# Fourier stage, first part: the next tile's join between centring and scaling, folds in pairs, GpSimd's roots in another order

## Chip, core and metric

The kernel runs on one core of a Trainium2 chip. The metric is the time of one execution in device microseconds; lower is better. The engines are TensorE (PE in the profile), VectorE (DVE), ScalarE (ACT), GpSimd (POOL) and SyncE (SP), which issues most transfers. Each engine works off its own queue of instructions in order and waits for others by semaphores.

## What is computed

Two layers of a diffusion trunk on 1024 tokens of width 1024, each with a token mixer and a mixture of experts. Layer 0 mixes by windowed attention, layer 1 by a Fourier transform. The change is in the Fourier stage of layer 1, and in its first part only. What that part computes, for x of 1024 x 1024:

```python
def post_norm(x, y, g, b):                     # end of layer 0: y is the summed output of its experts
    z = DEEPNORM_ALPHA * x.astype(jnp.float32) + y.astype(jnp.float32)
    return (_normalize(z, LN_EPS) * g.astype(jnp.float32) + b.astype(jnp.float32)).astype(x.dtype)

def modulate(x, shift, scale):                 # start of layer 1
    return (_normalize(x, MOD_EPS) * (1.0 + scale.astype(jnp.float32)) + shift.astype(jnp.float32)).astype(x.dtype)

def fourier_mixer(u, w_f):
    B, L, D = u.shape
    ug = u.reshape(B, L, F_GROUPS, D // F_GROUPS).astype(jnp.float32)
    f = jnp.fft.fft2(ug, axes=(1, 3), norm='ortho').real
    return f.reshape(B, L, D).astype(u.dtype) @ w_f

        x = post_norm(x, g2 * y2, ln_g[i, 1], ln_b[i, 1])
        u = modulate(x, sh1, sc1)
        y = fourier_mixer(u, fnet_w[j])
```

## The kernel before

The tokens lie in eight tiles of 128 rows. `TURN` orders them so that tiles 2j and 2j + 1 of the order are those whose rows are half the sequence apart; the transform over the tokens works on their sum and difference. All loops are unrolled, and the order of the instructions on each engine is the order in which they are written out. For tile i of the order the first part does this:

- SP: `load(i)` fetches the two partial sums of the experts from memory into one of three buffers `y[i % 3]`; from the fourth on it waits until that buffer has been read.
- TensorE: `total(i)` adds the partial sums into the one PSUM area `psY` (L278; for the first two tiles L276 too); it waits until the tile before has been joined.
- VectorE: *join* (L2189) forms z = ALPHA * x + psY in the one buffer `z`; *statistics* (L2190 to L2193) end with the variance, on which GpSimd's `root1` (L2147) works; *centring* (L2194) is (z - mean) * gain; *scaling* (L2196) waits for the root and writes x, with the row sums.
- ScalarE: `mean(i)` (L2256, L2258) takes the mean from these sums and the sum of squares; GpSimd's `root2` (L2152, L2154) makes the second root of it in two instructions; `normal(i)` (L2263, L2265) writes u, one of four buffers.
- VectorE: `fold(k)` (L2182) writes the sum (k even) or the difference (k odd) of the two u of a pair into `pm`; both folds of a pair want both u.
- TensorE: `turn(k)` (L2344) transposes a fold into the one area `psT`; ScalarE: `turned(k)` (L2270) copies it out; TensorE: `features(k)` (L2355) multiplies it by the feature table, in two halves; ScalarE: `features(k)` (L2275) copies each half to F.

Between these stands work on the condition's rows: TensorE's `rows(q)` and `columns()`, on ScalarE `rows(q)` (a copy, L2237 to L2242, for q = 1, 2 with a transfer issued from ScalarE's queue, L2245), `columns()` (L2227 to L2231, which scales the feature table that features(0) reads) and `spread`. The last tile's u is made on VectorE (`normalise`, L297 to L304). The second part (from L2383 on) multiplies F by the token tables and begins when all of F is there.

VectorE's order before is: for tile i join, statistics, centring, scaling, fold(i - 2). GpSimd's is: root2(i - 1), then root1(i). ScalarE's for tile i is: mean(i), columns at i = 1, turned(i - 2), normal(i), features(i - 3), rows(i - 1) at i = 2 and 3. TensorE's from i = 2 on is: total(i + 1), rows(2) at i = 2, turn(i - 2), features(i - 3).

## Time and profile before

| what | us |
|---|---|
| median of 3 runs (2733.79 to 2737.6) | 2733.92 |
| the profiled execution, its own time | 2736.14 |
| its span, first to last instruction | 2734.3 |
| Fourier stage in it, 1545.0 to 1663.6 | 118.6 |
| its first part, until the last features matmul ends | 1545.0 to 1624.6 |
| TensorE busy in the whole span | 2622.8 (96%) |
| VectorE busy in the whole span | 2021.4 (74%) |

The times of single instructions below count from the start of the span. In the views of instructions in order of time a line gives the start, the duration, the engine, the line of the kernel, the operation, the tile written and the tiles read; in brackets stands the idle time of the engine just before it and the engine that ended it. `f_banks` is the PSUM, `f_feat` is F or `pm`, `wide_t` holds z and u, `f_ny` and `wide_w` hold what was transposed.

### The profile page before, as it was taken

How to read it: one execution, taken by the hardware profiler on the slowest of the kernel's cores; microseconds unless marked ns; L12 is line 12 of the kernel's file. 1: busy time of each engine (PE TensorE's matmuls, PEld its weight loads, DVE VectorE, ACT ScalarE, POOL GpSimd, SP SyncE). 2: the span in 40 equal slices, each digit the busy share in tenths (PEclk: the TensorE clock that was granted, in tenths of full speed). 3: DMA queues.
4: the chain of work that ended last, by engine and by line, in shares of the span. 5: the costliest groups of instructions: out<-in, count | busy, mean ns of one | idle time of the engine just before them, and what ended most of it. 6: DMA issues, size and time to landing. Idle time of an engine off the chain costs nothing. (4 is left out here: it accounts for less than half of the span.)

```text
span 2734.3 us, 44521 instructions
## 1 busy us (share of the span) xinstructions
PE 2622.8 (96%) x14898; PEld 1188.5 (43%) x14899; DVE 2021.4 (74%) x5305; ACT 1367.1 (50%) x3178; POOL 615.0 (22%) x467
## 2 busy tenths in 40 slices
PE   7999999999899999999999889998999999999996
PEld 2444666545433333333444365454333333333342
DVE  4996666585588888788888555755898888888875
ACT  1113666343166666666666241432666666666651
POOL 0000000111023333233322221100233323333322
PEclk9999999999999999999999999999999999999998
DMA  9776500200399999999999732015999999999996
GB/s 376 253 267 198 187 17 17 76 39 39 130 378 367 335 333 353 324 334 377 353 337 335 253 138 88 34 47 228 356 363 345 334 320 338 331 377 336 331 356 206
DMA packets 151614, 697.66 MB, mean 255 GB/s; under 512 B 25504, under 2 KB 30880, under 8 KB 99161
## 3 DMA queue, kind: packets, MB, share of 16 engines
q1 hardware_dynamic: 104252, 556.14, 52.1%
q0 software_dynamic: 46832, 136.58, 20.2%
q8 instruction: 119, 1.95, 0.3%
q10 hardware_dynamic: 304, 2.11, 0.2%
q14 instruction: 107, 0.88, 0.1%
HBM read 597.50 MB, written 129.13 MB: 266 GB/s over the span
## 5 line engine op out<-in xcount | busy, mean ns | idle before, releaser
L1811 ACT ACTIVATE xT<-xt_blocks 32x256 f32<-32x256 f32 x2208 | 913.6, 414 | 40.2 <-DVE xt_blocks L1636 12.6
L1888 PE MATMUL exG<-ring,xT 128*32 128x512 f32 (+2 forms) x2608 | 572.2, 594 | 0.8 <-DMA ring<-in_exp_w_up_dram 0.8
L1651 DVE STREAM_TRANSPOSE ex_hT<-ex_h 32x64 f32<-32x64 f32 x2240 | 528.7, 236 | 33.6
L1888 PE MATMUL exG<-wide_w,xT 128*32 128x512 f32 (+2 forms) x1472 | 387.5, 601 | 0.0
L1561 POOL DMA_INDIRECT y_scratch<-wide_w,idx_out x203 | 337.2, 1661 | 165.0 <-issue 80.1
L1888 PE MATMUL exG<-wide_t,xT 128*32 128x512 f32 (+2 forms) x960 | 360.2, 602 | 11.2 <-issue 7.6
L1548 POOL DMA_INDIRECT wide_t<-u_scratch,idx x144 | 152.8, 1061 | 923.7 <-DVE idx_out L1685 779.1
L1888 PEld LDWEIGHTS exG<-ring,xT 128*32 128x32 f32 (+2 forms) x2608 | 199.3, 130 | 315.9 <-issue 311.7
L1823 ACT ACTIVATE ex_e<-exG 128x256 f32<-128x256 f32 x142 | 54.4, 383 | 513.7 <-PE exG L1888 513.7
L1922 PE MATMUL exD<-ring,ex_hT 128*32 128x512 f32 (+2 forms) x1304 | 296.2, 597 | 2.6 <-DVE wide_w L1677 2.5
L1641 DVE TENSOR_TENSOR ex_h<-ex_e,exG 128x256 f32<-128x256 f32 x142 | 86.9, 612 | 167.3 <-ACT ex_e L1823 165.0
L1888 PEld LDWEIGHTS exG<-wide_w,xT 128*32 128x32 f32 (+2 forms) x1472 | 133.6, 135 | 147.6 <-issue 147.6
L1922 PE MATMUL exD<-wide_w,ex_hT 128*32 128x512 f32 (+2 forms) x736 | 197.4, 597 | 0.0
L1677 DVE SCALAR_TENSOR_TENSOR wide_w<-exD,w_all,mod 128x1024 f32<-128x1024 f32 x142 | 182.3, 1284 | 9.4 <-PE exD L1922 8.4
L1888 PEld LDWEIGHTS exG<-wide_t,xT 128*32 128x32 f32 (+2 forms) x960 | 111.3, 136 | 166.8 <-issue 163.3
L1922 PE MATMUL exD<-wide_t,ex_hT 128*32 128x512 f32 (+2 forms) x480 | 182.0, 597 | 0.0
L1600 DVE TENSOR_TENSOR mod<-place,slots 128x1024 bf16<-128x1024 f32 (+3 forms) x203 | 175.2, 889 | 5.0 <-PEq L235 3.6
L1636 DVE STREAM_TRANSPOSE xt_blocks<-wide_t 128x1024 f32<-128x1024 f32 x138 | 170.8, 1237 | 1.6 <-DMA wide_t<-u_scratch,idx 1.6
L795 DVE TENSOR_REDUCE mx<-pair 128x1 f32<-128x640 f32 (+1 forms) x128 | 100.6, 787 | 94.4 <-PE pair L923 94.4
L315 POOL TENSOR_TENSOR rstd<-var,halves 128x1 f32<-128x1 f32 x42 | 62.9, 1498 | 441.1 <-DVE var L301 441.1
L1922 PEld LDWEIGHTS exD<-ring,ex_hT 128*32 128x32 f32 (+2 forms) x1304 | 97.0, 129 | 116.8 <-issue 115.6
L1241 ACT ACTIVATE u2T<-mod 32x256 f32<-32x256 f32 x224 | 92.7, 414 | 107.1 <-DVE mod L1115 104.5
(367 smaller groups left out, 3293.8 us busy)
## 6 DMA issues: line engine op xcount, KB each, us to landing
ring<-in_exp_w_gate_dram SPq DMA_DIRECT2D x64, 1024.0 KB
ring<-in_exp_w_up_dram SPq DMA_DIRECT2D x64, 1024.0 KB
ring<-in_exp_w_down_dram SPq DMA_DIRECT2D x64, 1024.0 KB, 14.2
wide_t<-in_exp_w_gate_dram SPq DMA_DIRECT2D x34, 1024.0 KB
wide_t<-in_exp_w_up_dram SPq DMA_DIRECT2D x34, 1024.0 KB
wide_t<-in_exp_w_down_dram SPq DMA_DIRECT2D x34, 1024.0 KB, 14.5
wide_w<-in_exp_w_gate_dram SPq DMA_DIRECT2D x32, 1024.0 KB
wide_w<-in_exp_w_up_dram SPq DMA_DIRECT2D x32, 1024.0 KB
```

Source lines behind the costliest of these rows:

```text
L795: dve.tensor_reduce(mx[:, p % 2, j:j + 1], halves_of(p, pair[p % 2])[j], AX, ALU.max).then_inc(own, 1)
L1241: last = act.activation(uT[m * UNIT:(m + 1) * UNIT, t % DEEP, :, a * UNIT:(a + 1) * UNIT], parts[a * UNIT:(a + 1) * UNIT, m], ACT.Copy)
L1548: pool.indirect_dma_start(out=xg[:, par], out_offset=None, in_=u_dram, in_offset=bass.IndirectOffsetOnAxis(ap=idx[:, par:par + 1], axis=0) ...
L1561: pool.indirect_dma_start(out=y_dram[layer], out_offset=bass.IndirectOffsetOnAxis(ap=idx_out[0:at + n, par, j:j + 1], axis=0), in_=yo[0:at ...
L1600: last = dve.tensor_tensor(hot[:, par, :, at:at + n], place[:, :, r:r + 1].to_broadcast([P, NT, n]), slots[:, start:start + n].unsqueeze(1 ...
L1636: dve.transpose(xt[:], xg[:, par]).then_inc(blocks_done, 1)
L1641: dve.tensor_tensor(hid[:, par].rearrange("t (k p) -> t p k", k=FK), e[:].rearrange("t (p k) -> t p k", k=FK), psG[par][:, 1].rearrange("t ...
L1651: last = dve.transpose(hT[m * UNIT:(m + 1) * UNIT, par].rearrange("p (k t) -> p k t", k=FK)[:, :, a * UNIT:(a + 1) * UNIT], hid[a * UNIT:( ...
L1677: dve.scalar_tensor_tensor(out=yo[:, par], in0=psD[:].rearrange("p a b -> p (a b)"), scalar=w_all[:, ds(b, 1)], in1=gate2, op0=ALU.mult, o ...
L1811: last = act.activation(xT[m * UNIT:(m + 1) * UNIT, par, :, a * UNIT:(a + 1) * UNIT], parts[a * UNIT:(a + 1) * UNIT, m], ACT.Copy)
L1888: last = pe.matmul(psG[par][p:p + m], xT[:, par, k, p:p + m], ring[s % RING][:, 0:2, k * FF:(k + 1) * FF], start=k == 0, stop=k == KT - 1)
L1922: last = pe.matmul(psD[p:p + m, c], hT[:, b % 2, k * P + p:k * P + p + m], ring[s % RING][:, 2, k * D + c * 512:k * D + (c + 1) * 512], st ...
```

## The change

VectorE now joins tile i + 1 between the centring and the scaling of tile i (for i = 1 behind the scaling). For this z has two buffers, and the row of the bias that lay in one of them moves to the last u buffer. Two semaphores, `z_joined` and `z_mid`, replace two of the four links per tile. The folds come in pairs behind the scaling of tiles 2, 4 and 6. GpSimd does root1(i) ahead of root2(i - 1). SP issues load(3) ahead of sums(2) and load(4) ahead of the tables. ScalarE's queue goes by pairs: mean(i), turned(i - 2), normal(i), turned(i - 1), features(i - 2), then mean(i + 1), normal(i + 1), features(i - 1); both columns() and the first two tiles' normal come ahead of it, rows(1) and rows(2) behind features(0). TensorE's goes by pairs too: turn(k), total(k + 4), turn(k + 1), features(k), total(k + 5), features(k + 1).

```diff
-                z, u, pm = fT[:, 3], fT[:, 4:4 + U], F[:, 6:8]
+                z, u, pm = [fT[:, 0], fT[:, 3]], fT[:, 4:4 + U], F[:, 6:8]
...
-                bias_a, bias_b = fT[:, 0], F[:, 1:6].rearrange("p t d -> p (t d)")
+                bias_a, bias_b = fT[:, 7], F[:, 1:6].rearrange("p t d -> p (t d)")
...
                         load(2)
+                        load(3)
                         sums(2)
-                        load(3)
+                        load(4)
                         for buf, name in ((even_c, "even_c"), (odd_c, "odd_c"), (even_s, "even_s")):
                             sp.dma_start(buf[:].rearrange("p a b -> p (a b)"), A[name]).then_inc(t_in, 16)
-                        for i in range(4, NT):
+                        for i in range(5, NT):
                             load(i)
...
                         add_last(pool, layer, held)
-                        for i in range(NT):
-                            if i >= 1:
-                                root2(i - 1)
+                        root1(0)
+                        for i in range(1, NT):
                             root1(i)
+                            root2(i - 1)
                         root1(NT)
...
-                        for i, t in enumerate(TURN):
-                            link = Links(dve, own, i * 4)
-                            after(dve, x_done, i, 1)
+                        def joined(i):
+
                             dve.wait_ge(y_mm, i + 1)
-                            xs = x[:, t]
-                            link(stt(out=z, in0=xs, scalar=ALPHA, in1=flat(psY), op0=ALU.mult, op1=ALU.add))
-                            dve.bn_stats(r["st"][:, 0, :], z[:, 0:512])
-                            link(dve.bn_stats(r["st"][:, 1, :], z[:, 512:1024]))
+                            at_least(dve, x_done, i - 1)
+                            stt(out=z[i % 2], in0=x[:, TURN[i]], scalar=ALPHA, in1=flat(psY), op0=ALU.mult, op1=ALU.add).then_inc(z_joined, 1)
+
+                        def centred(i):
+
+                            link = Links(dve, own, i * 2)
+                            dve.wait_ge(z_joined, i + 1)
+                            dve.bn_stats(r["st"][:, 0, :], z[i % 2][:, 0:512])
+                            link(dve.bn_stats(r["st"][:, 1, :], z[i % 2][:, 512:1024]))
                             link(dve.bn_aggr(r["mv"][:], r["st"][:]))
                             dve.tensor_scalar(r["var"][:], r["mv"][:, 1:2], LN_EPS, None, ALU.add).then_inc(r["asked"], 1)
-                            link(stt(out=z, in0=z, scalar=r["mv"][:, 0:1], in1=lnp[:, 0], op0=ALU.subtract, op1=ALU.mult))
+                            stt(out=z[i % 2], in0=z[i % 2], scalar=r["mv"][:, 0:1], in1=lnp[:, 0], op0=ALU.subtract, op1=ALU.mult).then_inc(z_mid, 1)
+
+                        def scaled(i):
+
+                            dve.wait_ge(z_mid, i + 1)
                             dve.wait_ge(r["ready"], i + 1)
-                            stt(out=xs, in0=z, scalar=r["rstd"][:], in1=lnp[:, 1], op0=ALU.mult, op1=ALU.add, accum_out=sm[:, i:i + 1]).then_inc(x_done, 1)
-                            if i >= 2:
+                            stt(out=x[:, TURN[i]], in0=z[i % 2], scalar=r["rstd"][:], in1=lnp[:, 1], op0=ALU.mult, op1=ALU.add,
+                                accum_out=sm[:, i:i + 1]).then_inc(x_done, 1)
+
+                        joined(0)
+                        for i in range(NT):
+                            centred(i)
+                            if i != 1 and i + 1 < NT:
+                                joined(i + 1)
+                            scaled(i)
+                            if i == 1:
+                                joined(2)
+                            if i >= 2 and i % 2 == 0:
                                 fold(i - 2)
-                            assert link.n == 4
+                                fold(i - 1)
...
                         rows(0)
-                        for i in range(NT):
-                            if i < NT - 1:
-                                mean(i)
-                            if i == 1:
-                                columns()
+                        for i in range(2):
+                            mean(i)
+                            normal(i)
+                        columns()
+                        for i in range(2, NT, 2):
+                            mean(i)
+                            turned(i - 2)
+                            normal(i)
+                            turned(i - 1)
+                            features(i - 2)
+                            if i == 2:
+                                rows(1)
+                                rows(2)
                             if i == 6:
                                 spread(1)
                                 spread(2)
-                            if i >= 2:
-                                turned(i - 2)
-                            if i < NT - 1:
-                                normal(i)
-                            if i >= 3:
-                                features(i - 3)
-                            if i in (2, 3):
-                                rows(i - 1)
+                            if i + 1 < NT - 1:
+                                mean(i + 1)
+                                normal(i + 1)
+                            features(i - 1)
                         turned(NT - 2)
-                        features(NT - 3)
                         turned(NT - 1)
...
-                            if i >= 1:
-                                pe.wait_ge(own, 4 * (i - 1) + 1)
+                            at_least(pe, z_joined, i)
                             add_sums(pe, psY, pairs, y[i % 3], layer, TURN[i], held).then_inc(y_mm, 1)
...
-                        for i in range(2, NT):
-                            if i + 1 < NT:
-                                total(i + 1)
-                            if i == 2:
-                                rows(2)
-                            turn(i - 2)
-                            if i >= 3:
-                                features(i - 3)
+                        total(3)
+                        rows(2)
+                        for k in range(0, NT - 2, 2):
+                            turn(k)
+                            if k + 4 < NT:
+                                total(k + 4)
+                            turn(k + 1)
+                            features(k)
+                            if k + 5 < NT:
+                                total(k + 5)
+                            features(k + 1)
                         turn(NT - 2)
-                        features(NT - 3)
                         turn(NT - 1)
```

## Rows read from the trace of the kernel before

**Rows 1.** Busy us of each engine by stretches; then granted clock, DMA share, GB/s.
```profile
1565.00:1607.00 42.00, 34.42 (x176) 20.14 (x168) 36.85 (x54) 29.78 (x52) 12.91 (x17) 0.95 0.51 194
1607.00:1625.00 18.00, 16.81 (x88) 14.50 (x88) 5.44 (x8) 7.64 (x11) 0.55 (x1) 1.00 0.00 0
...
1579.00:1581.00 2.00, 2.00 (x9) 1.73 (x7) 1.92 (x4) 1.33 (x3) 0.55 (x1) 0.53 0.10 38
```

**Rows 2.** Waits from 1545 to 1610: who for whom, us, times, longest.
```profile
DVE x L2196 <- POOL rstd L2147: 4.9, 8, 1.3
```

**Rows 3.** VectorE in order of time: join of tile 2; tile 6, join to fold.
```profile
1563.86 1.22 DVE L2189 SCALAR_TENSOR_TENSOR wide_t<-x,f_banks 128x1024 f32<-128x1024 f32 x1 [1.18 <-PE f_banks L278]
...
1593.59 1.21 DVE L2189 SCALAR_TENSOR_TENSOR wide_t<-x,f_banks 128x1024 f32<-128x1024 f32 x1
...
1596.47 1.28 DVE L2194 SCALAR_TENSOR_TENSOR wide_t<-wide_t,mean_var,wide_w 128x1024 f32<-128x1024 f32 x1
1598.26 1.28 DVE L2196 SCALAR_TENSOR_TENSOR x<-wide_t,rstd,wide_w 128x1024 f32<-128x1024 f32 x1 [0.51 <-POOL rstd L2147]
...
1599.47 1.22 DVE L2182 TENSOR_TENSOR f_feat<-wide_t 128x1024 f32<-128x1024 f32 x1
```

**Rows 4.** GpSimd in order of time: root2 and root1; the last root1.
```profile
1594.13 0.19 POOL L2152 TENSOR_SCALAR u_ss<-u_ss 128x1 f32<-128x1 f32 x1 [2.99 <-ACT wide_t L2258]
1594.41 0.55 POOL L2154 TENSOR_TENSOR u_rstd<-u_ss,halves 128x1 f32<-128x1 f32 x1
1596.64 1.52 POOL L2147 TENSOR_TENSOR rstd<-var,halves 128x1 f32<-128x1 f32 x1 [1.68 <-DVE var L2193]
...
1609.52 0.55 POOL L2147 TENSOR_TENSOR rstd<-var,halves 128x1 f32<-128x1 f32 x1 [4.35 <-DVE var L301]
```

**Rows 5.** All engines in order of time, in the finish stage.
```profile
2726.28 1.29 DVE L2032 SCALAR_TENSOR_TENSOR fx<-fz,z_rstd,mod 128x1024 f32<-128x1024 f32 x1
2726.38 1.59 POOL L2009 TENSOR_TENSOR z_rstd<-z_ss,halves 128x1 f32<-128x1 f32 x1
```

**Rows 6.** ScalarE in order of time: columns, rows' issues, mean, turned, normal, features.
```profile
1565.25 3.30 ACT L2231 ACTIVATE feat_scaled<-feat,f_scale 128x256 f32<-128x256 f32 x8
...
1575.44 1.07 ACTq L2245 DMA_DIRECT2D row_scratch<-odd_s  x1
...
1585.82 0.49 ACTq L2245 DMA_DIRECT2D row_scratch<-odd_s  x1
...
1592.57 0.20 ACT L2256 ACTIVATE u_nmean<-u_sum 128x1 f32<-128x1 f32 x1 [1.01 <-DVE x L2196]
1592.80 1.15 ACT L2258 ACTIVATE wide_t<-x,u_nmean 128x1024 f32<-128x1024 f32 x1
...
1594.86 1.02 ACT L2270 ACTIVATE wide_w<-f_banks 128x1024 f32<-128x1024 f32 x1 [0.81 <-PE f_banks L2344]
1595.78 0.29 ACT L2263 ACTIVATE u_shift<-u_nmean,u_rstd 128x1 f32<-128x1 f32 x1
1596.10 1.24 ACT L2265 ACTIVATE wide_t<-x,u_shift,u_rstd 128x1024 f32<-128x1024 f32 x1
1597.25 0.57 ACT L2275 ACTIVATE f_feat<-f_banks 128x512 f32<-128x512 f32 x1
```

**Rows 7.** TensorE in order of time: total(3), turns, features, and the second part's start.
```profile
1567.06 1.94 PE L278 MATMUL f_banks<-wide_w,pairs 128*64 128x512 f32 x8
...
1578.35 1.26 PE L2344 MATMUL f_banks<-ident,f_feat 128*128 128x128 f32 x8 [3.61 <-DVE f_feat L2182]
1579.39 5.18 PE L2355 MATMUL f_banks<-feat_scaled,f_ny 128*128 128x256 f32 x16
...
1607.76 1.09 PE L2344 MATMUL f_banks<-ident,f_feat 128*128 128x128 f32 x8 [2.47 <-DVE f_feat L2182]
...
1620.95 3.62 PE L2355 MATMUL f_banks<-feat_scaled,wide_w 128*128 128x256 f32 x16
1625.35 1.03 PE L2383 MATMUL f_banks<-even_c,f_feat 128*4 128x257 f32 x4 [0.78 <-ACT f_feat L2275]
```

More of the change, by code:

```diff
@@ L2099, in fourier @@
                 paired, y_mm, own, x_done = (sem(n) for n in ("paired", "y_summed", "fin_own", "x_done"))
+                z_joined, z_mid = sem("z_joined"), sem("z_mid")
                 y_in, ln_in = summed_in[layer], norm_in
```

## The prediction, made before the result was known

> **What bounds the kernel now.** I first read the busy time by stretches [rows 1]. The Fourier stage runs from 1545 to 1663.6 us of the span. In its first part, from 1565 to 1607, VectorE is busy 36.85 of 42 us and TensorE 34.42; from 1607 to 1625 VectorE has 5.44 of 18 left and TensorE 16.81. So the first part goes at VectorE's pace and hands over to a TensorE tail. Everything behind waits for the last features matmul, which starts at 1620.95 and ends at 1624.57: the second part's first matmul, at 1625.35, was released by ScalarE's copy of it [rows 7]. A microsecond there is a microsecond of the whole.
>
> Next VectorE's steady tile in order of time [rows 3]: join at 1593.59, behind it the statistics, centring at 1596.47, a wait of 0.51 for GpSimd's root, scaling at 1598.26, fold at 1599.47. From start to start that is 2.88 for join and statistics (1.22 of it the join), 1.79 for centring with the wait, 1.21 for scaling, and some 1.15 for the fold: 7 us a tile. The table of waits puts all eight root waits at 4.9 us [rows 2]. That is what the change can take away, at 0.5 to 0.6 a tile; it is no large prize.
>
> Why does the root take so long? It takes 1.52 while centring runs beside it (1596.47 to 1597.74, root until 1598.16) and 0.55 when nothing does [rows 3, 4]. The finish stage shows the same for a scaling: GpSimd starts at 2726.38, the scaling at 2726.28 ends at 2727.57, and the root takes 1.59, until 2727.97 [rows 5]. A root that meets centring or scaling ends 0.41 after that instruction. The sum below uses this.
>
> The Trainium skill ("SBUF — State Buffer", Who interferes with whom) says that a VectorE instruction with two SBUF inputs and a GpSimd one that reads SBUF exclude each other, whoever came first. GpSimd as the loser is in the rows; VectorE as the loser is not shown by any. By that rule scaling of tile 5 would be held about 0.1 more and the sum would be 3.7 instead of 3.6.
>
> **The parts of the change and their cost.** I lay the queues out in their new order with durations of the rows. TensorE: total 1.94, turn 1.09, features 3.62 [rows 7]. ScalarE: mean 1.5 (copy at 1592.57, square from 1592.80, GpSimd following at 1594.13), turned 1.02, normal 1.55 (1595.78 to 1597.34), each half of the features copy 0.6, eight column scalings 3.3 with two small ones of 0.2 in front of them [rows 4, 6]. GpSimd's second root: 0.83 from 1594.13 to its end at 1594.96 [rows 4]. Handing over from engine to engine costs 0.03 to 0.12. The same layout with the old orders gives 1624.4 for the last features matmul, against 1624.57 in the trace, so it is good to some 0.2 us.
>
> *Removed and nearly free.* The link waits in the join and centring cost nothing once another instruction stands between. The second z buffer and the bias row's new place cost nothing: only the first row sums read that bias, ahead of total(2), and its place, u of tile 3, is first written at about 1585 in the sum below. On SP load(3) passes sums(2), and load(4) passes the tables. This costs nothing: total(3) at 1567.06 shows no wait for a transfer [rows 7], rows(2), which reads sums(2), comes behind total(3), and total(4) comes 0.9 later than in the layout of the old orders. The row staging moves back to 1584.8, and the load of the last table, which waits for it on SP, with it; the table is wanted behind the last features matmul, 40 us later, and those 40 us are the cover. Without it the whole delay of the staging would count.
>
> *Tiles 2 and 3.* Join(2) still waits for data until 1563.86 [rows 3]. Centring ends at 1568.0. Join(3) now wants total(3) before scaling(2), but that ends at 1567.06 + 1.94 = 1569.0: VectorE waits 1.1, where it waited 0.51 for the root. Scaling(2) ends at 1571.6, folds 0 and 1 at 1573.8, join(4) and scaling(3) at 1579.2. The statistics of tile 4 start at 1579.0, against 1579.5 in the layout of the old orders. Gain so far 0.5.
>
> *Tiles 4 and 5.* On ScalarE normal(1) ends at 1570.8: its root2 stands behind root1(2) on GpSimd, which is held by centring until 1568.4. Behind it come columns (to 1574.4), mean(2) (to 1575.8) and turned(0) (to 1576.9), which before stood in another order. TensorE's turn(1) waits for turned(0), so features(0) runs 1577.8 to 1581.5 and total(5), behind it in the new order, ends at 1583.2. Centring(4) ended at 1581.9, so join(5) waits 1.5. Scaling(4) ends at 1585.9. Now the costly step: fold(2) needs u of tile 3, whose mean is queued on ScalarE behind features(0) (copied by 1582.1) and the two row stagings with their transfer issues (two copies of 0.6, issues of 1.07 and 0.49 [rows 6]; to 1584.8). Mean(3) ends at 1586.3, root2 at 1587.2, normal(3) at 1588.8. Fold(2) starts at 1588.85: VectorE waits 2.9. Queued behind it are fold(3), centring(5), and for TensorE turn(2).
>
> *Tiles 6 and 7.* From 1588.85 two folds (to 1591.2), centring(5), join(6) and scaling(5) to 1596.5, centring(6) to 1599.3, total(7) just in time, scaling(6) 1600.55 to 1601.9. On ScalarE normal(4) ends at 1596.9 (root2(4) waits for root1(5), which centring holds until 1594.4), turned(3) at 1597.8, the copies of features(2) at 1598.9, mean(5) at 1600.3. Its second root reaches the power at 1600.7, in the middle of scaling(6), and ends at 1602.3; normal(5) ends at 1603.9. Fold(4) starts at 1604.0: VectorE waits 2.0.
>
> *Tail.* Folds 4 and 5 end at 1606.3, root1(7) at 1609.55, scaling(7) at 1611.0, the last normalisation lets fold(6) start at 1614.4. Root2(6) stands behind root1(7), and its power is then held by scaling(7): 1611.4. Normal(6) ends at 1613.0, turned(5) behind it at 1614.0, one copy of features(4) at 1614.5; only then features(5) runs, to 1618.15. Turn(6), turned(6) and turn(7) end at 1621.3, features(6) and (7) at 1628.2. Sum: 1628.2 - 1624.57 = 3.6 us later.
>
> In short: tiles 2 to 6 give back their root waits, some 3, and a join wait of the old order goes (1.3 in its layout); the new waits (1.1, 1.5, 2.9, 2.0) take 7.5; the tail adds a little. Unknown costs: the power under scaling (nothing to 1.1 on each of three: held nowhere, the layout gives 1.6 later instead of 3.6; with no holding even by centring, 1.1 earlier); the transfer issue on ScalarE (0 to 1.6: 0.6 less if nothing). I take the held value, since its row is the same form of instruction [rows 5].
>
> The profiled execution took 2736.14 around a span of 2734.3; its sum becomes 2739.7. The median of the three runs is 2733.92, lower by 2.2, and I add the 3.6 to it: 2737.5.
>
> **Rivals.** (A) The sum: 2737.5, with 2735.5 to 2738.5 for the unknown costs.
>
> (B) GpSimd's new order doesn't bind, because the second roots come before the first ones ask. The layout with the old order of roots shows what that is worth: normal(1) is done at 1566, fold(2) at 1587.7, features(5) at 1609.2, and the end is 1.5 earlier than before: 2732.4. For it: a second root is 0.83 long and mostly idle time surrounds it. Against: root1 of the next tile is asked about 2 us after scaling and centring then holds it, so it must come first by order.
>
> (C) The other side, clearly slower: TensorE's clock. After a pause of 3.61 us turn(1) took 1.26 and features(0) 5.18 instead of 3.62 [rows 7], the granted clock being 0.53 (between its levels of 2.4 and 1.2 GHz) from 1579 to 1581 [rows 1]. A pause of 2.47 at 1607.76 had no such end. In the new order there are pauses of 2.4 before turn(4) and again before features(5), and 3.3 before turn(2). A fall there costs 1.6 for each features that stands on the path: features(0) and features(5) do. One gives 2739.1, both 2740.7, slower by more than 0.2%. It decides if two of them fall.
>
> (D) The change doesn't reach the end: the delays are taken up by slack in the tail or behind the stage. 2734. Against: no slack is seen in front of 1620.95 or behind 1625.
>
> **Chances.** A 0.55, B 0.2, C 0.2, D 0.05. A change of 0.2%, 5.5 us, is about what a measurement of this kernel can tell from none. A, B, D and half of C lie inside it, though A is a small loss. Faster by more 0.03 (B with all the waits gone), slower by more 0.18 (C with both, or more of it), within 0.79. The range goes from B's 2732.4 to a little beyond C's 2740.7: 2732 to 2741.5.
>
> **What would show it.** Right: VectorE's join of tile 5 waits 1 to 2 us for TensorE's sums; folds 2 and 4 wait 2 to 4 us each for ScalarE's normal; scalings 2 to 6 wait for no root; the second roots of tiles 0, 5 and 6 take about 1.6 instead of 0.55; the last features matmul ends 3 to 4 us later. Wrong: folds that start right behind their scaling (then ScalarE isn't the limit, and B is nearer), 0.55 for all second roots, or 5 us for features(5) or (0) (C).

## The result and the profile after

The change made the kernel slower: 2743.51 us (median of 20 executions) beside 2735.97 for the kernel before (median of 20 on the same chip). The ratio is 1.0023 with a 95% interval of 1.0015 to 1.0031, so about 6.3 us more (4.1 to 8.5); the two medians alone differ by 7.5. The prediction was 2737.5 with a range of 2732 to 2741.5; the time lies outside it.

| in the profiled execution, us | before | after |
|---|---|---|
| its own time | 2736.14 | 2742.53 |
| its span | 2734.3 | 2740.7 |
| start of the Fourier stage | 1545.26 | 1546.59 |
| first part, until the last features matmul ends | 79.31 | 83.06 |
| second part | 39.09 | 39.12 |
| all that follows | 1070.64 | 1071.93 |

Of 6.4 us between the two spans the first part has 3.75. The other 2.6 lie ahead of the stage and behind it, where no instruction changed. One place of these is a stretch of the finish stage in which TensorE's granted clock was 0.72; that falls of the clock make up all of the 2.6 isn't added up here. Over all the profiles below the stage starts between 1542.9 and 1548.0 and what follows takes 1069.2 to 1073.7, with no order by kernel.

The busy time by stretches of the kernel after (us, then the busy time of TensorE, its weight loads, VectorE, ScalarE and GpSimd, then granted clock, DMA share, GB/s): the stretches that answer to [rows 1], then two places in the first part, then the one in the finish stage.
```profile
1569.00:1611.00 42.00, 35.18 (x166) 20.99 (x165) 33.40 (x47) 28.02 (x50) 12.22 (x16) 0.89 0.31 115
1611.00:1630.00 19.00, 15.46 (x78) 12.95 (x76) 6.11 (x9) 8.77 (x13) 2.17 (x3) 1.00 0.29 110
...
1574.00:1578.00 4.00, 4.00 (x16) 1.33 (x14) 3.58 (x6) 3.97 (x9) 1.46 (x1) 0.61 0.74 295
1590.00:1596.00 6.00, 4.24 (x16) 2.15 (x16) 5.11 (x7) 3.77 (x7) 1.46 (x1) 0.72 0.05 20
...
2696.00:2702.00 6.00, 4.78 (x10) 1.16 (x12) 0.22 (x1) 0.00 (x0) 1.57 (x1) 0.72 0.40 48
```
VectorE is busy 33.4 of 42 us, against 36.85 in [rows 1]: its waits have grown. The table of VectorE's waits, 1545 to 1618, says for whom (total, times, longest):
```profile
DVE wide_t L2190 <- PE f_banks L278: 11.2, 6, 6.0
DVE f_feat L2184 <- ACT wide_t L2285: 4.0, 3, 3.2
...
DVE x L2206 <- POOL rstd L2149: 1.0, 2, 0.5
```
The root waits went from 4.9 [rows 2] to 1.0, as the change means them to. In their place stand waits of folds for ScalarE's normal (4.0; before, 0.2) and of joins for TensorE's sums (11.2 against 6.8). Of the 11.2, though, 7.4 belong to joins 0 and 1 at the entry of the stage; joins 2 to 7 have 3.8, against 2.4 in the kernel before. In order of time on VectorE (joins 4 and 5, folds 2 and 3, join 6, join 7, scaling 6, folds 4 and 5, folds 6 and 7):
```profile
1578.43 1.22 DVE L2190 SCALAR_TENSOR_TENSOR wide_t<-x,f_banks 128x1024 f32<-128x1024 f32 x1 [0.78 <-PE f_banks L278]
...
1584.85 1.22 DVE L2190 SCALAR_TENSOR_TENSOR wide_t<-x,f_banks 128x1024 f32<-128x1024 f32 x1 [1.17 <-PE f_banks L278]
...
1590.48 2.36 DVE L2184 TENSOR_TENSOR f_feat<-wide_t 128x1024 f32<-128x1024 f32 x2 [3.21 <-ACT wide_t L2285]
...
1596.40 1.22 DVE L2190 SCALAR_TENSOR_TENSOR wide_t<-x,f_banks 128x1024 f32<-128x1024 f32 x1 [0.74 <-PE f_banks L278]
...
1602.74 1.22 DVE L2190 SCALAR_TENSOR_TENSOR wide_t<-x,f_banks 128x1024 f32<-128x1024 f32 x1 [1.10 <-PE f_banks L278]
1603.88 1.28 DVE L2206 SCALAR_TENSOR_TENSOR x<-wide_t,rstd,wide_w 128x1024 f32<-128x1024 f32 x1
...
1605.37 2.36 DVE L2184 TENSOR_TENSOR f_feat<-wide_t 128x1024 f32<-128x1024 f32 x2 [0.20 <-ACT wide_t L2285]
...
1615.84 2.36 DVE L2184 TENSOR_TENSOR f_feat<-wide_t 128x1024 f32<-128x1024 f32 x2
```
Why folds 2 and 3 wait 3.21 is seen on ScalarE, in order of time: the second half of features(0), the two row copies with their transfer issues, and only then mean(3), at 1586.46, with normal(3) behind it.
```profile
1582.97 0.60 ACT L2295 ACTIVATE f_feat<-f_banks 128x512 f32<-128x512 f32 x1 [1.00 <-PE f_banks L2377]
1583.46 0.59 ACT L2262 ACTIVATE odd_s<-f_banks 128x512 f32<-128x512 f32 x1
1584.08 1.07 ACTq L2265 DMA_DIRECT2D row_scratch<-odd_s  x1
1585.21 0.69 ACT L2260 ACTIVATE odd_s<-f_banks,f_consts 128x512 f32<-128x512 f32 x1 [1.15 <-issue]
1585.92 0.49 ACTq L2265 DMA_DIRECT2D row_scratch<-odd_s  x1
1586.46 0.20 ACT L2276 ACTIVATE u_nmean<-u_sum 128x1 f32<-128x1 f32 x1 [0.56 <-ACT odd_s L2260]
...
1589.21 1.24 ACT L2285 ACTIVATE wide_t<-x,u_shift,u_rstd 128x1024 f32<-128x1024 f32 x1
```
GpSimd's second roots of tiles 0, 5 and 6:
```profile
1564.41 1.43 POOL L2156 TENSOR_TENSOR u_rstd<-u_ss,halves 128x1 f32<-128x1 f32 x1
...
1603.19 0.55 POOL L2156 TENSOR_TENSOR u_rstd<-u_ss,halves 128x1 f32<-128x1 f32 x1
...
1611.32 1.44 POOL L2156 TENSOR_TENSOR u_rstd<-u_ss,halves 128x1 f32<-128x1 f32 x1
```
And TensorE, to compare with [rows 7]: total(4), turn(2) and total(6) behind its pause, features(5), and the last features matmul, which ends at 1629.65.
```profile
1574.78 3.61 PE L278 MATMUL f_banks<-wide_w,pairs 128*64 128x512 f32 x8
...
1591.76 1.82 PE L2366 MATMUL f_banks<-ident,f_feat 128*128 128x128 f32 x8 [3.31 <-DVE f_feat L2184]
1593.51 2.84 PE L278 MATMUL f_banks<-wide_w,pairs 128*64 128x512 f32 x8
...
1615.90 3.69 PE L2377 MATMUL f_banks<-feat_scaled,wide_w 128*128 128x256 f32 x16 [1.98 <-ACT f_feat L2295]
...
1626.03 3.62 PE L2377 MATMUL f_banks<-feat_scaled,wide_w 128*128 128x256 f32 x16
```
A total takes 1.94 at full clock [rows 7]; total(4) took 3.61 and total(6) 2.84. The granted clock beside them (0.61, 0.72) says why: it lay between its levels of 2.4 and 1.2 GHz, that is, a part of the stretch ran at the lower one.

### The profile page after: what moved, and what is told of

Read it like the earlier page. It is cut to its first block and busy times, and to the rows that moved or that the text cites. A ratio compares the mean times of both kernels' runs of the same rounds, so it can differ in the third digit from the quotient of the medians.

```text
span 2740.7 us, 44518 instructions
## 1 busy us (share of the span) xinstructions
PE 2630.1 (96%) x14896; PEld 1192.2 (44%) x14899; DVE 2020.5 (74%) x5305; ACT 1366.3 (50%) x3178; POOL 615.9 (22%) x467
## 5 line engine op out<-in xcount | busy, mean ns | idle before, releaser
L1561 POOL DMA_INDIRECT y_scratch<-wide_w,idx_out x203 | 335.6, 1653 | 167.6 <-issue 82.9
```

What stands on the lines that cost most here:

```text
L1561: pool.indirect_dma_start(out=y_dram[layer], out_offset=bass.IndirectOffsetOnAxis(ap=idx_out[0:at + n, par, j:j + 1], axis=0), in_=yo[0:at ...
```

## The experiments

Three theories are weighed in the expectations, in these or other words. **Queues:** the new orders of GpSimd and ScalarE make VectorE and then TensorE late, whatever the clock does. **Clock:** the order by pairs has more pauses of TensorE, each of which may be followed by a fall of its clock; the queues are minor. **Behind:** the stage is late by the sum alone, and the rest is lost behind it.

"Layout" below is the prediction's way of laying the queues out, with the entry of the stage as in the execution before (its total(2) took 3.68, at the lower clock) and every turn, features and later total at its full-clock duration. The layouts are worked out from the rows and stand in no view. "Time" is the ratio to the kernel before, run on the same chip, times the latter's median, with the 95% interval (it isn't the difference of the two medians, which lies up to 1.8 away). "First part" is from one profile each, two of the kernel before. "Clock" is the mean of the granted clock over all timed executions of that kernel; 0.001 of it is 2.7 us of full-clock time, of which a part falls into pauses and costs nothing.

| kernel | time, us more than before | first part, us | layout | clock (executions) |
|---|---|---|---|---|
| before | 0 | 79.3, 79.2 | 78.1 | 0.9852 (32), 0.9851 (35) |
| after | +6.3 (4.1 to 8.5) | 83.1 | 82.9 | 0.9838 (20) |
| e1_after | +6.0 (3.6 to 8.2) | 85.9 | 82.9 | 0.9839 (11) |
| e2_old_roots | +4.1 (1.4 to 6.8) | 84.5 | 77.9 | 0.9837 (12) |
| e3_new_roots_alone | +7.1 (3.8 to 10.1) | 85.7 | 84.7 | 0.9838 (8) |
| e4_scalar_order | -0.8 (-3.6 to 1.9) | 79.4 | 78.9 | 0.9853 (12) |
| e5_both | -2.2 (-4.9 to 0.8) | 79.7 | 76.4 | 0.9850 (11) |
| e6_delay | +4.7 (1.9 to 7.4) | 85.4 | | 0.9842 (12) |
| e7_old_roots_busy | +10.1 (7.1 to 13.4) | 88.8 | | 0.9851 (12) |
| e8_both_busy | +5.2 (2.7 to 7.7) | 82.7 | | 0.9853 (11) |
| e10_old_roots_fill | +1.4 (-1.9 to 4.7) | 77.7 | | 0.9860 (12) |
| e11_both_fill | -3.0 (-5.7 to 0.0) | 77.5 | | 0.9863 (11) |
| e12_after_fill | +3.0 (0.0 to 6.3) | 82.1 | | 0.9858 (12) |

**The changed kernel again**, without an edit.

> The changed kernel once more. Two theories. Queues: the first part of the Fourier stage (from VectorE's first instruction of the stage to the end of the last features matmul; 79.3 us in the profile of before, 83.1 in that of the change) is longer by 3.6 us because of the order of GpSimd's roots and of ScalarE's queue, and the rest of the measured difference (about 6 us) is falls of TensorE's clock elsewhere, which come and go. It expects 83.1 again within 0.4, and falls of the clock outside the stage in other places than in the first profile. Clock: the change itself brings falls, in its pauses and behind them; it expects the lost clock time of the profile (38 us before, 45 with the change) to be about 45 again, at the same places, and 6 us more than before in time.

The time repeats (+6.0), the first part doesn't: 85.89 instead of 83.06, where the theory of the queues expected 83.1 within 0.4. Total(4), turn(2) and total(6) are slow again, the last two more so (1.97 and 3.68, against 1.82 and 2.84 in the first profile), and features(5) is slow for the first time. TensorE in order of time and the stretch around it, in this execution:
```profile
1618.26 5.38 PE L2377 MATMUL f_banks<-feat_scaled,wide_w 128*128 128x256 f32 x16 [1.98 <-ACT f_feat L2295]
```
```profile
1618.00:1622.00 4.00, 3.74 (x12) 3.08 (x13) 2.52 (x3) 1.20 (x3) 0.00 (x0) 0.68 1.00 420
```
This is features(5) behind a pause of 1.98, just as in the first profile, where it took 3.69; here it took 5.38. The same pause is once followed by a fall and once not.

**The change with GpSimd's old order.**
```diff
-                        root1(0)
-                        for i in range(1, NT):
+                        for i in range(NT):
+                            if i >= 1:
+                                root2(i - 1)
                             root1(i)
-                            root2(i - 1)
```

> The change with GpSimd's old order of roots (second root of a tile ahead of the next tile's first). Queues: the layout by the rows gives a first part 1.3 us shorter than before (78.0) and 5.1 shorter than the change; folds 2 and 4 start right behind their scaling or within 0.3 us. Clock as the cause: the pauses of TensorE stay about as they are, so 81 to 83 and a time within 2 us of the change. Should the order of roots not matter: 83.

By its layout this first part is 77.9; it took 84.5. The queues did what was laid out: folds wait for no normal. The late mean(3) still holds VectorE, for 3.39, but now at scaling(4), since root1(4) stands behind root2(3) in the old order. The loss against the layout is TensorE's. VectorE and TensorE in order of time:
```profile
1587.64 1.28 DVE L2206 SCALAR_TENSOR_TENSOR x<-wide_t,rstd,wide_w 128x1024 f32<-128x1024 f32 x1 [3.39 <-POOL rstd L2149]
```
```profile
1572.64 3.68 PE L278 MATMUL f_banks<-wide_w,pairs 128*64 128x512 f32 x8
...
1607.77 1.94 PE L2366 MATMUL f_banks<-ident,f_feat 128*128 128x128 f32 x8 [1.47 <-ACT f_ny L2290]
1609.51 4.39 PE L2377 MATMUL f_banks<-feat_scaled,f_ny 128*128 128x256 f32 x16
```
Total(4) took 3.68 instead of 1.94, turn(5) 1.94 instead of 1.09, features(4) 4.39 instead of 3.62; total(3) and total(6) were slow too (3.42, 3.10). With TensorE's measured durations in it the layout gives 84.3 instead of 77.9. So the clock took what the queues gave; and the fall at turn(5) came after a pause of 1.47 only. By the expectation this run alone speaks for the clock as the cause; the queues' part of it is shown only with the pauses filled, below.

**The kernel before with GpSimd's new order alone.** The edit is the one above in the other direction.

> The kernel before with nothing but GpSimd's new order of roots. Queues: the layout gives 5.6 us more than before, a first part of 84.9, folds waiting some 2 us each for ScalarE's normal, and about 0.2% in time. If the loss lies in ScalarE's and TensorE's order by pairs and the roots are innocent: 79.3 as before and no change in time.

Here the two theories are far apart, and the queues win: nothing else is changed, no folds are in pairs, and the first part is 6.4 longer than before (6.6 in the layouts). VectorE and GpSimd in order of time, fold(2) and the second root in front of it:
```profile
1586.24 1.23 DVE L2182 TENSOR_TENSOR f_feat<-wide_t 128x1024 f32<-128x1024 f32 x1 [2.03 <-ACT wide_t L2265]
```
```profile
1583.17 1.44 POOL L2154 TENSOR_TENSOR u_rstd<-u_ss,halves 128x1 f32<-128x1 f32 x1
```
Every second root of tiles 0 to 6 falls under a scaling and takes 1.43 or 1.44, where [rows 4] has 0.55, and three folds wait 2.0 to 2.4 for ScalarE.

**The change with another order on ScalarE:** the mean of the pair's second tile ahead of the copies of features(i - 2), and the row stagings behind normal(3).
```diff
                             turned(i - 1)
+                            if i + 1 < NT - 1:
+                                mean(i + 1)
                             features(i - 2)
-                            if i == 2:
-                                rows(1)
-                                rows(2)
...
                             if i + 1 < NT - 1:
-                                mean(i + 1)
                                 normal(i + 1)
+                            if i == 2:
+                                rows(1)
+                                rows(2)
                             features(i - 1)
```

> The change with its new order of roots, and with ScalarE's order mended only: mean of the odd tile ahead of the copies of features(i - 2), the row stagings behind that tile's normal. The layout gives 78.9 us for the first part at full clock, where the change has 82.9 in the layout. Falls of the clock in the pauses have cost 0 to 6.5 on top in the runs so far, 3 on the mean: 79 to 84 in one profile, and 0 to 3 us more than before in time. If GpSimd's order alone makes the loss, 83 and more, and 5 us or more in time.

The whole loss is gone: first part 79.4, time -0.8. ScalarE and VectorE in order of time, mean(3), and scaling(4) with folds 2 and 3 behind it:
```profile
1579.95 0.19 ACT L2276 ACTIVATE u_nmean<-u_sum 128x1 f32<-128x1 f32 x1
```
```profile
1584.24 1.28 DVE L2206 SCALAR_TENSOR_TENSOR x<-wide_t,rstd,wide_w 128x1024 f32<-128x1024 f32 x1
1585.45 2.35 DVE L2184 TENSOR_TENSOR f_feat<-wide_t 128x1024 f32<-128x1024 f32 x2
```
Counted from the start of the stage, mean(3) comes 4.9 earlier than in the changed kernel, and the fold starts right behind its scaling. GpSimd's new order is still in here. So neither order alone makes the loss in the changed kernel: it takes both, and undoing either is enough for the queues (78.9 and 77.9 in the layout, against 78.1 before).

**Both orders undone**, that is e2 and e4 together.

> The change with the old order of roots and with ScalarE's mean of the odd tile ahead of the copies of features(i - 2), the row stagings behind that tile's normal. Queues: the layout gives 76.5 us for the first part, 2.8 less than before and 6.6 less than the change, so 0.1% faster than before. Clock as the cause: no shorter than 80.

By its layout 76.4, which would be 1.7 less than before; it took 79.7 by falls again (total(4) 3.68, features(4) 5.31). The time is 2.2 less than before, and its interval holds no change.

**The kernel before with a delay:** three chained additions on VectorE in front of fold(6), whose result nothing uses.
```diff
+                        for n in range(3):
+                            link(tt(z, x[:, TURN[0]], x[:, TURN[1]], ALU.add))
                         fold(NT - 2)
```

> The kernel before with three more additions of 1.2 us on VectorE, each waiting for the one ahead of it, in front of fold(6): a pure delay of about 3.7 us in the tail and nothing else. If a delay of the stage simply adds to the time, the first part is 83.0 and the time 3.7 us more than before. If a longer stage also brings falls of TensorE's clock behind it (the profiles of the change showed 2 to 4 us more of lost clock behind the stage than that of before), the time is 5 to 8 us more and the stretch behind the stage is 1072 us as in the change and not 1070.6 as before.

They took 3.74; the first part became 6.1 longer, and what follows took 1069.4, no more than elsewhere. In this profile the theory "behind" falls: a delay ahead of the tail reaches the end whole, and nothing is lost after it. The timed executions, +4.7 with 1.9 to 7.4, can't tell 3.7 from 5 to 8. Of the other 2.4, 1.7 is a new fall at features(5); the rest lies ahead of the additions. In order of time on TensorE:
```profile
1617.51 1.09 PE L2346 MATMUL f_banks<-ident,f_feat 128*128 128x128 f32 x8 [3.58 <-DVE f_feat L2182]
1618.44 5.31 PE L2357 MATMUL f_banks<-feat_scaled,wide_w 128*128 128x256 f32 x16
```

**Pauses filled, first try.** On e2 and on e5 TensorE gets matmuls whose result nothing reads, into an unused bank, in front of turns 0, 2 and 5 (0 and 5 on e5).
```diff
+            BUSY = {0: 6, 2: 8, 5: 6}
...
+                            for _ in range(n):
+                                pe.matmul(banks[:, bank], ident[:], lnp[:, 0, 0:512], start=True, stop=True)
```

> The run with the change and the old order of roots, with matmuls that nothing reads in TensorE's pauses (6 of 512 columns ahead of turn(0), 8 ahead of turn(2), 6 ahead of turn(5)). Clock: the layout at full clock gives 77.9 us for the first part where 84.5 was measured; with the pauses filled the falls in the stage from turn(0) on go, and the first part comes to 78 to 80. If the layout was wrong for another reason than the clock: 84.5 or, the fill being work, more.

> The run with both orders mended (first part 79.7 measured, 76.4 in the layout at full clock), with the same fill ahead of turn(0) and turn(5). Clock: 76.4 to 78 for the first part, and some 4 us less than before in time, 0.15%. If the fill only costs: 80 or more.

Both are slower, because the fill was sized wrongly: six such matmuls take 5.42, more than the pauses of 1.67 and 1.47 that e2 had ahead of turns 0 and 5. In order of time on TensorE (e7_old_roots_busy):
```profile
1572.53 5.42 PE L2365 MATMUL f_banks<-wide_w,ident 128*128 128x512 f32 x12
1577.78 1.04 PE L2377 MATMUL f_banks<-ident,f_feat 128*128 128x128 f32 x8
```
What they do show: from turn(0) on neither has an instruction at the lower clock, and the mean clock is back at that of the kernel before.

**The kernel before again.** One execution, to see how much the falls in it vary.

> The kernel before once more, for its falls of the clock. If they come by chance, they lie partly in other places than in the first profile of before, also ahead of the stage, where nothing differs; the first part stays within 1.7 us of 79.3. If they are fixed to the kernel: the same places and 79.3.

The first part took 79.2, with the same falls as in the first profile (total(2) 3.68, and features(0) as shown); ahead of the stage they lay partly in other places.
```profile
1577.01 5.22 PE L2355 MATMUL f_banks<-feat_scaled,f_ny 128*128 128x256 f32 x16
```

**Pauses filled, right size:** 256 columns instead of 512, two to six at a place, on e2, on e5 and on the changed kernel.
```diff
+            BUSY = {('turn', 0): 3, ('turn', 2): 4, ('turn', 5): 3, ('total', 3): 3}      # e10
+            BUSY = {('turn', 0): 3, ('turn', 5): 3, ('total', 3): 3}                      # e11
+            BUSY = {('turn', 0): 3, ('turn', 2): 6, ('turn', 4): 4, ('turn', 5): 2, ('total', 3): 2, ('features', 5): 4}  # e12
```

> The change with the old order of roots and a fill of TensorE's pauses, now sized to fit them: matmuls of 256 columns that nothing reads, 0.85 us for two, 3 each ahead of total(3), turn(0) and turn(5) and 4 ahead of turn(2). (In the first fill one matmul of 512 columns took 0.86 us and the fill of 5 us outlasted the pauses of 1.5 to 3.) Clock: the layout's 77.9 up to 79.5, against 84.5 without the fill, no falls between total(3) and the last features matmul. If the pauses have nothing to do with the falls: 84 with falls in the same places.

> Both orders mended, with 3 matmuls of 256 columns ahead of total(3), turn(0) and turn(5). Clock: 76.4 by the layout up to 77.5 for the first part, against 79.7 without the fill and 79.3 before; 2 to 4 us less than before in time. If the fill only costs: 80 or more.

> The changed kernel itself with its pauses filled (2 matmuls of 256 columns ahead of total(3), 3 ahead of turn(0), 6 ahead of turn(2), 4 ahead of turn(4), 2 ahead of turn(5), 4 ahead of features(5)): the share of the two causes. The queues alone give 82.9 by the layout; with the clock kept up the first part is 82.5 to 84 and the time 3.5 to 4.5 us more than before, 2 us less than the change has. If the whole loss were the clock's, the first part would come to 79 or 80 and the time to that of before.

The stretches of e10_old_roots_fill and of e12_after_fill, entry of the stage and all behind it:
```profile
1546.00:1550.00 4.00, 3.66 (x7) 0.95 (x8) 0.24 (x2) 0.00 (x0) 1.58 (x1) 0.58 0.55 107
1550.00:1626.00 76.00, 67.98 (x343) 41.54 (x344) 53.24 (x77) 42.67 (x72) 16.89 (x24) 1.00 0.48 175
```
```profile
1544.70:1548.00 3.30, 3.05 (x6) 0.80 (x6) 0.21 (x2) 0.00 (x0) 1.58 (x1) 0.54 0.69 111
1548.00:1627.00 79.00, 70.65 (x356) 44.09 (x352) 53.31 (x77) 41.55 (x72) 19.68 (x23) 1.00 0.45 166
```
Behind the entry the clock is at 1.00 in both. So these two show the queues without the clock: with the old roots the first part takes 77.7, where the layout says 77.9; the change as it is takes 82.1, where it says 82.9 and 82.5 to 84 was expected. (The entry isn't the layout's: total(2) took 1.94 in both and not 3.68, so agreement to some tenths is partly luck.) Whole times are less sharp: e10 isn't faster than the kernel before (+1.4, -1.9 to 4.7), and the +3.0 of e12 and the +6.0 of e1 have intervals that overlap. In e12_after_fill the fold still waits for ScalarE, while features(5), with its pause filled, keeps its clock (VectorE, then TensorE, in order of time):
```profile
1588.60 2.36 DVE L2185 TENSOR_TENSOR f_feat<-wide_t 128x1024 f32<-128x1024 f32 x2 [3.21 <-ACT wide_t L2286]
```
```profile
1613.02 3.69 PE L2391 MATMUL f_banks<-feat_scaled,wide_w 128*128 128x256 f32 x16
```
In e10_old_roots_fill no fold waits, and the late mean(3) is paid at scaling(4) on VectorE:
```profile
1587.12 1.29 DVE L2207 SCALAR_TENSOR_TENSOR x<-wide_t,rstd,wide_w 128x1024 f32<-128x1024 f32 x1 [3.40 <-POOL rstd L2150]
```
Side by side, these two tell where the new order of roots costs. From the start of the stage, folds 2 and 3 begin at 42.3 with the old roots and 43.9 with the new, folds 4 and 5 at 55.7 and 57.8, folds 6 and 7 at 66.2 and 68.3, and the last features matmul ends at 77.7 and 82.1. So of the 4.4 between the two about half arises behind the last folds: with the new roots normal(6) is late, and turned(5) and the copy that features(5) waits for stand behind it on ScalarE. The 3.21 at folds 2 and 3 is the largest wait, but not the largest loss.

e11_both_fill has the shortest time of all, 2733.68 beside 2736.58, but its interval reaches 1.0000, so that it beats the kernel before is likely and not settled. No run filled the pauses of the kernel before, so the 78.1 of the queues alone in it is a layout and was not measured.

## Why the prediction was wrong

**The queues' part was right, and its end in absolute time close.** The prediction let the last features matmul end at 1628.2, that is 82.9 behind the stage's start at 1545.26. It took 83.06 in the first profile, 85.89 in the second and 82.1 with the pauses filled; that the first lies within 0.2 is luck. The mechanism stands: normals that are late on ScalarE and GpSimd hold VectorE and then TensorE, shown by e4 (ScalarE's order undone: nothing left), e2 with e10 (GpSimd's undone: 77.7) and e3 (GpSimd's alone: enough for a loss).

**The step that failed first is the falls of TensorE's clock in the new order, which the sum put at nothing.** The 1624.57 that the sum takes off holds a fall: features(0) took 5.18 [rows 7], total(5) behind it came late, and join(5) waited for it, in order of time on VectorE of the kernel before:
```profile
1586.57 1.22 DVE L2189 SCALAR_TENSOR_TENSOR wide_t<-x,f_banks 128x1024 f32<-128x1024 f32 x1 [1.26 <-PE f_banks L278]
```
This is the "join wait of the old order" that the prediction lets go. The new order was laid out at full clock throughout, so the forecast took a fall away and put none in its place. At full clock on both sides the old order ends at 1545.26 + 78.05 = 1623.3, and the change costs 82.9 - 78.05 = 4.9. The fall at features(0) does go: it took 5.18, 5.22 and 5.30 in before, e9 and e6, and 3.62 in all profiles of the order by pairs. But others come. Total(4) took 2.49 to 3.68 instead of 1.94 in all five of these without a fill, at no cost in the layout of the change, where turn(1) waits for ScalarE meanwhile. Turn(2) and total(6) took together 4.7 and 5.7 in the two profiles of the change, laid out at 3.0, and features(5) 5.38 in the second.

**The second is the chance of C, and that it was a rival at all.** C priced a fall at 1.6 and asked for two of them at features(0) and features(5). A fall did come at features(5), in e1, of 5.38 - 3.69 = 1.7. But falls don't stand in place of the sum; they come on top of it, in the kernel before as well. With the measured durations of TensorE in place of the full-clock ones, the layout gives 79.3 for before, 82.9 for after, 85.8 for e1, 84.3 for e2, 86.0 for e3 and 80.0 for e5, where 79.3, 83.1, 85.9, 84.5, 85.7 and 79.7 were measured. The clock's share, the difference to the full-clock layouts of the table, is thus 1.3, 0.0, 2.9, 6.5, 1.3 and 3.6. That the first pair of profiles differs by 3.75, near the predicted 3.6, is chance: in the one a fall cost 1.3, and in the other the falls at total(4), turn(2) and total(6) cost on balance nothing, since total(2) took 1.94 there and not the 3.68 of the layout. Over the timed executions the change lowers the mean clock from 0.9852 to 0.9838 and 0.9839, 3.6 to 3.8 us of full-clock time more, of which a part costs nothing. Read back from the two profiles, 4.9 less 1.3 and plus 0.0 to 2.9 is 3.6 to 6.5 more; 6.3 and 6.0 were measured.

**The third is the base.** The prediction took 2733.92, the median of three. Over 20 to 35 executions the kernel before has 2735.97 to 2737.07. It had the number against it in hand: the profiled execution's own 2736.14. So of the 6.0 us by which it missed, 2.05 are the base; with 2735.97 as base the same range would have reached to 2743.55, just above the 2743.51 measured. Of the other 4.0, 1.3 is the step from the ratio's 6.3 to the 7.5 between the medians. The remaining 2.7 is what 6.3 has beyond 3.6. That falls of the clock can be part of it is shown by the second profile beside the filled one (85.9, 82.1); what share of it they are, and what the spread of the executions, isn't settled by these runs.

**The single steps.**
- Scalings 2 to 6 wait for no root: right, 1.0 us are left of 4.9.
- Join(3) waiting 1.1: wrong, it didn't wait, since total(2) ran earlier and at full clock (in e4, where total(2) took the layout's 3.68, it waited 1.09); join(4) waited 0.78 instead, for the slow total(4).
- Join(5) waiting 1.5: right in kind, 1.17.
- Fold(2) waiting 2.9 for ScalarE behind features(0) and the row stagings: right, 3.21, and in both further profiles of this order again 3.21.
- Fold(4) waiting 2.0: off, 0.20. VectorE lost the time just ahead of it, in joins 6 and 7 (0.74 and 1.10), for totals that the late fold and the clock had delayed; the three together are 2.04. With the clock kept up (e12) they were nothing, 0.30 and 0.83, so here part of the loss is the clock's.
- Second roots of tiles 0, 5 and 6 held by scalings: 1.43 and 1.44 for tiles 0 and 6, but 0.55 for tile 5: scaling(6), late behind join(7), began at 1603.88, when that root was done.
- Tail: folds 6 and 7 start 69.25 behind the stage's start, laid out 69.1; features(5) waits 1.98 for ScalarE's copy behind turned(5), as laid out. In the kernel before these folds start 65.7 behind the stage's start, so against it the tail adds 0.2 of the 3.75, little as predicted; the tail's share above is against the old roots in the new order.

**The rivals.** B falls as stated: the new root order binds. Its price for the old order was good (77.7 to 77.9 against its 77.8), though the clock kept that gain out of reach in e2. D falls by e6. C was right that falls follow the new pauses, and had too low a chance: its condition, falls at features(0) and features(5) both, was met in no profile of the change, but falls elsewhere, which it didn't price, came in both.

On the held roots the Trainium skill ("SBUF — State Buffer", Who interferes with whom) agrees with the runs for GpSimd as the one that waits: 1.43 to 1.44 under a scaling, 0.55 alone, and the scalings beside them took the same 1.28 as all others. VectorE as the one that waits is again shown by no row.

## What to carry to other kernels

When a wait of 0.5 us is taken from the busiest engine by reordering, follow the moved instruction through the in-order queues of the helpers: here a mean that went behind two copies and two transfer issues on ScalarE, together with a root that went behind another on GpSimd, cost more than all the waits saved. Set a layout against a layout, both at the same clock, never against an execution that holds a fall; add the falls as a term of their own with its spread, and take the base from many executions. That folds in pairs as such lower TensorE's clock is not shown: e4 and e5 keep them and have the mean clock of the kernel before (0.9853, 0.9850). Without a fill, the lowest mean clocks (after and its repetition e1, e2, e3; 0.9837 to 0.9839) belong to the orders in which VectorE waits 2 us and more for a late root or normal, and e3 of them has no pairs. So the queues' waits are likely to bring the falls with them; by these runs that is a pattern and not proved.

## What the runs showed of the hardware

- Pauses of 1.5 to 2 us were followed by falls of TensorE's clock (1.47 ahead of turn(5) in e2, 1.98 ahead of features(5) in e1), while the same 1.98 in the first profile was not, nor 1.94 ahead of turn(5) in e4, nor 2.47 ahead of turn(5) in the kernel before. A fall whose slow stretch was all work cost 1.7 us (total(4): 3.68 instead of 1.94; features(5): 5.38 instead of 3.69).
- Matmuls whose result nothing reads, sized to the pause, kept the granted clock at 1.00 over 76 and 79 us (e10, e12), and took 6.8 us off the first part of e2 (84.5 to 77.7) and 1.0 and 3.8 off those of the change (83.1 and 85.9 to 82.1), one profile each. Sized too long, they cost more than the falls.
- One f32 matmul of 512 columns stands as two records in the trace: six are listed as x12 and take 5.42 us, 0.9 each. Three of 256 columns are listed as x6 and take 1.46 to 1.56 us (e10).
- The two transfers issued from ScalarE's queue behind the row copies held ScalarE for 1.07 and 0.49 us. Two later ones in the changed kernel (0.36 and 0.44 us, from 1613.96 on) lay beside running instructions and held nothing.
